# Probabilities turned by VectorE and Pool's DMAs through DRAM in a two-layer hybrid block

## The reference, cut to what matters

```
s_loc = where(ok, q @ k_loc.T * scale + bias, NEG);  s_ctx = q @ k_ctx.T * scale
p = softmax(concat([s_loc, s_ctx(, sink)]))          # rows: queries, columns: keys
o = p[:, :n_loc] @ v_loc + p[:, n_loc:] @ v_ctx
```

## Time and profile before

| What | us |
|---|---|
| median of 3 runs | 1846.57 (1845.81 to 1846.89) |
| span of the profiled execution | 1846.3 |
| TensorE busy in it | 1689.6 (92%) |
| VectorE busy | 771.0 (42%) |
| ScalarE busy | 478.0 (26%) |
| Pool busy | 111.4 (6%) |
| attention of layer 0 | about 148 to 424 |
| expert stage of layer 0 | about 580 to 1080 |
| attention of layer 1 | about 1130 to 1314 |
| expert stage of layer 1 | about 1397 to the end |

### The profile page before, as it was taken

How to read it: one execution, slowest core, us unless ns; L and a number is a source line. 1 busy time by engine, 2 the same in 40 slices (tenths; PEclk the granted TensorE clock), 3 DMA queues, 4 the chain that set the end, 5 groups by cost and what they waited for, 6 DMA issues and landing times.

```text
span 1846.3 us, 26514 instructions
## 1 busy us (share of the span) xinstructions
PE 1689.6 (92%) x10854; PEld 977.2 (53%) x10854; DVE 771.0 (42%) x1746; ACT 478.0 (26%) x1052; POOL 111.4 (6%) x149
## 2 busy tenths in 40 slices
PE   5999999999998999999898799989999997777866
PEld 2887777777674333333232398877883332222222
DVE  3455556674434233333323665577753222111111
ACT  3324455552223100000000434465441000000001
POOL 1001210000001000000000101300001000000000
PEclk8999999999998999999999999999998999999998
DMA  9532322127778999999999764337899999999996
GB/s 353 154 91 69 106 72 80 35 81 256 251 286 326 409 428 427 428 428 428 427 429 426 271 206 133 96 115 252 282 364 385 426 426 426 426 425 426 426 426 281
DMA packets 152035, 543.83 MB, mean 295 GB/s; under 512 B 10026, under 2 KB 92400, under 8 KB 126700
## 3 DMA queue, kind: packets, MB, share of 16 engines
q1 hardware_dynamic: 149104, 535.35, 74.0%
q0 software_dynamic: 2400, 6.16, 1.2%
q10 hardware_dynamic: 412, 0.64, 0.1%
HBM read 539.13 MB, written 2.98 MB: 294 GB/s over the span
## 4 chain that ended last, share of the span: by engine, by line
PE 68%; DMA 23%; DVE 4%; ACT 2%; SPq 2%; issue 1%; POOL 0%; DVEq 0%; ACTq 0%
PE bank L2158 20%; PE bank L2019 12%; PE bank L2020 11%; PE bank L2021 11%; DMA ring<-in_w_exp_down 8%; DMA ring<-in_w_exp_gate 7%; DMA ring<-in_w_exp_up 4%; DMA spare<-in_w_exp_gate 3%; PE bank L2132 2%; PE bank L2048 2%; PE bank L2071 2%; PE bank L1934 2%; PE bank L2058 2%; PE bank L2187 1%; DMA ring<-in_w_ada 1%
## 5 line engine op out<-in xcount | busy, mean ns | idle before, releaser
L2158 PE MATMUL bank<-ring,XEP 128*32 128x256 f32 (+1 forms) x2384 | 384.9, 617 | 37.1 <-DMA ring<-in_w_exp_gate 20.7
L2019 PE MATMUL bank<-HH,WH 128*128 128x512 f32 (+1 forms) x864 | 312.1, 361 | 5.7 <-DVE HL L1627 4.7
L2020 PE MATMUL bank<-HL,WH 128*128 128x512 f32 (+1 forms) x864 | 300.4, 348 | 0.0
L2021 PE MATMUL bank<-HH,WL 128*128 128x512 f32 (+1 forms) x864 | 299.9, 347 | 0.0
L2158 PEld LDWEIGHTS bank<-ring,XEP 128*32 128x32 f32 (+1 forms) x2384 | 114.1, 130 | 277.5 <-issue 227.8
L1598 DVE TENSOR_TENSOR WL<-ring,WH 128x1024 fp32r<-128x1024 f32 (+1 forms) x172 | 185.0, 1078 | 133.4 <-ACT WH L1362 132.6
L1856 DVE TENSOR_TENSOR X<-X,bank 128x512 f32<-128x512 f32 x184 | 114.0, 682 | 188.2 <-PE bank L2187 100.0
L2019 PEld LDWEIGHTS bank<-HH,WH 128*128 128x128 f32 x864 | 163.8, 190 | 54.0 <-issue 25.9
L1362 ACT CAST WH<-ring 128x1024 fp32r<-128x1024 f32 (+1 forms) x172 | 158.0, 926 | 100.5 <-PE bank L2021 64.7
L2158 PE MATMUL bank<-ring,HIDT 128*32 128x256 f32 (+1 forms) x1232 | 153.6, 481 | 31.3 <-DMA ring<-in_w_exp_down 31.3
L2021 PEld LDWEIGHTS bank<-HH,WL 128*128 128x128 f32 x864 | 163.8, 190 | 21.2
(11 more groups left out here) (244 smaller groups left out, 1955.4 us busy)
## 6 DMA issues: line engine op xcount, KB each, us to landing
ring<-in_w_exp_gate SPq DMA_DIRECT2D x55, 2048.0 KB, 30.9
ring<-in_w_exp_up SPq DMA_DIRECT2D x49, 2048.0 KB, 34.4
ring<-in_w_exp_down SPq DMA_DIRECT2D x48, 2048.0 KB, 36.6
ring<-in_w_ada SPq DMA_DIRECT2D x48, 1024.0 KB, 7.4
ring<-in_w_in SPq DMA_DIRECT2D x40, 1024.0 KB, 6.3
split_slot<-in_w_exp_up SPq DMA_DIRECT2D x8, 2048.0 KB, 29.3
split_slot<-in_w_exp_down SPq DMA_DIRECT2D x8, 2048.0 KB, 33.5
ring<-in_w_in SPq DMA_DIRECT2D x28, 512.0 KB, 5.2
```

Of the source, the lines that this page charges most:

```text
L2019: mm(t, wh, hi[:, k, 0:b.n], start=k == 0, stop=False)
L2020: mm(t, wh, lo[:, k, 0:b.n], start=False, stop=False)
L2021: last = mm(t, wl, hi[:, k, 0:b.n], start=False, stop=k == b.kk - 1)
L2158: last = mm(out_bank[tw * g:tw * g + tw, 0:nw], stationary(k), w[:, g::G] if spread else w[:, nw * g:nw * g + nw], start=k == 0, stop=k == ...
```

## The change

TensorE's transposes go. ScalarE scales PB by the reciprocal, in place, where VectorE did. A new step `swap` lets VectorE turn each 32x32 block of PB within itself and write it to a buffer PBT (one for both heads of a pair, in the last 1024 columns of the weight ring, which the ring gives up until the attention is over). Pool, at `turn`, writes PBT to one of two buffers in DRAM (`bounce`), waits until it has landed, and reads it back with four DMAs, one for each group of 32 partitions, so that the blocks lie where the transpose of the whole would put them, in PTL or PTC. TensorE waits for these DMAs (`pt_in`) before the values. The positions of the steps change: swaps come behind the normalising, values later (in layer 0 two pairs after the set's end, in layer 1 at 8/10 of the next pair's fill). Pool's bias steps are put in a new order by `bias_order`: one pair ahead in layer 0 and two in layer 1, then each next pair's behind the `turn` of a pair with a bias. The first pair of the last third of the merge does both gate blocks before the branch blocks.

```diff
         if place is None:
-            if self.top + size > STREAM[self.layer] * SLOT:
+            if self.top + size > STREAM[self.layer] * SLOT - self.kept:
                 self.top = 0
...
 
+        P.kept = PBT_W
...
@@ -582,7 +587,9 @@
                 at_ = [(both, lambda: normalise(pair[0])), (both, lambda: normalise(pair[1]))]
                 if br == "na" and last:
                     at_ = [(-(-per * 9 // 20), lambda: normalise(pair[0])), (-(-per * 7 // 10), lambda: normalise(pair[1]))]
-                at_ = sorted(at_ + [(-(-per * 3 // 10), values), (-(-per * 7 // 10), lower)], key=lambda a: a[0])
+                later = -(-per * 17 // 20) if br == "na" and last else both + 1
+                at_ += [(at_[1][0] if br == "na" and last else later, lambda: swap(pair[0])), (later, lambda: swap(pair[1]))]
+                at_ = sorted(at_ + [(-(-per * (8 if last else 4) // 10), lambda: values(pair[0].pair - (1 if last else 2))), (-(-per * (10 if last else 8) // 10), lower)], key=lambda a: a[0])
...
-
-            for st in P.turned:
-                P.add("pv", set=st)
-            P.lower += P.turned
-            P.turned = []
+        def swap(x):
+
+            P.add("swap", unit=x)
+
+        def values(until):
+
+            while P.turned and P.turned[0].end <= until + 1:
+                P.add("pv", set=P.turned[0])
...
+            P.add("turn", pair=pair)
+            if pair[1].end:
+                P.turned.append(pair[1].set)
...
-            run(atoms[:1 + KD // 2])
-            values()
-            run(atoms[1 + KD // 2:1 + KD])
-            lower()
-            run(atoms[1 + KD:mid])
+            if d2 == 0:
+                mid = 2 * KD + 3
+                atoms = atoms[:KD + 2] + atoms[KD + 8:2 * KD + 9] + atoms[KD + 2:KD + 8] + atoms[2 * KD + 9:]
+                done = 0
+                for n in (KD + 1, 2 * KD)[-len(P.turned):]:
+                    run(atoms[done:n])
+                    values(P.turned[0].end - 1)
+                    run(atoms[n:n + 3])
+                    lower()
+                    done = n + 3
+                run(atoms[done:mid])
+            else:
...
+        P.steps[l] = bias_order(out, 2 * (l + 1))
...
+def bias_order(steps, ahead):
+
+    due = [s for s in steps if s.kind == "bias"]
+    out = []
+
+    def pair():
+
+        now = [due.pop(0) for _ in range(2)] if due else []
+        out.extend(now + [Step(kind="mask", layer=s.layer, unit=s.unit) for s in now])
+
+    for s in steps:
+        if s.kind == "bias":
+            if s.unit.u == min(t.unit.u for t in steps if t.kind == "bias"):
+                for _ in range(ahead // 2):
+                    pair()
+            continue
+        out.append(s)
+        if s.kind == "turn" and s.pair[0].bias:
+            pair()
+    assert not due
+    return out
...
         RPBT = [sb(f"RPBT{l}", [8 * RPB_R, RPB_REP, RPB_C], R_O + 16384 + 8192 * l) for l in range(DEPTH)]
...
         MRG = [sb(f"MRG{l}", [128, KD, n], R_MRG) for l, n in enumerate((TOK, SEQ))]
-        PTL = sb("PTL", [128, 2, 4, SEQ], R_PT)
-        PTC = sb("PTC", [128, 2, 2, SEQ], R_PT + 8192)
+        PTL = sb("PTL", [128, 8, 2, 4, 32], R_PT)
+        PTC = sb("PTC", [128, 8, 2, 2, 32], R_PT + 8192)
+        PBT = [[sb(f"PBT{l}{nk}", [128, 4, 2, nk, 32], R_RING + 16384 * STREAM[l] - 4 * PBT_W) for nk in (4, 2)] for l in range(DEPTH)]
...
-        BLK, SB_, TB, PVB = BANK, BANK[3:5], BANK[5:7], BANK[7]
+        BLK, SB_, PVB = BANK, BANK[3:5], BANK[7]
...
+                    elif s.kind == "mask":
+                        mask(s.unit)
+                    elif s.kind == "turn":
+                        x = s.pair[1]
+                        pool.wait_ge(turn_ready, x.u + 1)
+                        run, held = 16 * x.nk // 32, bounce[x.pair % 2]
+                        if x.pair > 1:
+                            pool.wait_ge(pt_in, 64 * (x.pair - 1))
+                        pool.dma_start(held[:, 0:4 * run], PBT[l][x.set.grp][:].rearrange("p b h c j -> p (b h c j)")).then_inc(pt_out, 16)
+                        pool.wait_ge(pt_out, 16 * (x.pair + 1))
+                        if x.set.pt_before:
+                            pool.wait_ge(pv_ready, x.set.pt_before)
+                        j = x.qt % 2
+                        for b in range(4):
+                            blocks = bass.AP(tensor=held.tensor, offset=held.offset + run * b, ap=[[PBT_W, 32], [32 * PBT_W, 4], [1, run]])
+                            turned = (PTL, PTC)[x.set.grp][32 * b:32 * b + 32, 4 * j:4 * j + 4].rearrange("p a h c j -> p a (h c j)")
+                            pool.dma_start(turned, blocks).then_inc(pt_in, 16)
...
-                    elif kind == "turn":
+                    elif kind == "normalise":
                         x = s.unit
-                        act.wait_ge(turn_ready, x.u + 1)
-                        if x.set.pt_before:
-                            act.wait_ge(pv_ready, x.set.pt_before)
-                        buf, nk = (PTL, 4) if x.set.grp == 0 else (PTC, 2)
-                        j = x.qt % 2
-                        nc.scalar.copy(buf[:, x.hh, :, 128 * j:128 * j + 128],
-                                       TB[x.u % 2][:, 0:128 * nk].rearrange("p (k q) -> p k q", k=nk)).then_inc(pt_ready, 1)
+                        u2 = x.u % 2
+                        act.wait_ge(inverse_ready, x.u + 1)
+                        nc.scalar.activation(PB[u2][:, 0:x.nk], PB[u2][:, 0:x.nk], ACT.Copy, scale=RSM[u2]).then_inc(norm_ready, 1)
...
                                 link(nc.vector.tensor_reduce(MX[u2][:, 1:2], sc[:, SEQ:TOK], AX.X, ALU.max))
                                 nc.vector.tensor_reduce(NM[u2], MX[u2], AX.X, ALU.max, negate=True).then_inc(max_ready, 1)
                             elif x.br == "na":
-                                if x.u >= 2:
-                                    dve.wait_ge(turn_ready, x.u - 1)
                                 nc.vector.tensor_reduce(NM[u2], sc[:, 0:CTX], AX.X, ALU.max, negate=True).then_inc(max_ready, 1)
                             else:
-                                if x.u >= 2:
-                                    dve.wait_ge(turn_ready, x.u - 1)
                                 link(nc.vector.tensor_reduce(MX[u2][:, 0:1], sc[:, 0:CTX], AX.X, ALU.max))
...
-                        link(nc.vector.reciprocal(RSM[u2], RSM[u2]))
-                        nc.vector.tensor_scalar(PB[u2][:, 0:n], PB[u2][:, 0:n], RSM[u2], None, ALU.mult).then_inc(norm_ready, 1)
+                        nc.vector.reciprocal(RSM[u2], RSM[u2]).then_inc(inverse_ready, 1)
+                    elif kind == "swap":
+                        x = s.unit
+                        u2, n = x.u % 2, x.nk
+                        dve.wait_ge(norm_ready, x.u + 1)
+                        if x.hh == 0 and x.pair:
+                            dve.wait_ge(pt_out, 16 * x.pair)
+                        turned = PBT[l][x.set.grp][:, :, x.hh, :, :].rearrange("p b c j -> p c b j")
+                        nc.vector.transpose(turned, PB[u2][:, 0:n].rearrange("p (c b j) -> p c b j", b=4, j=32)).then_inc(turn_ready, 1)
...
                                     last.then_inc(s_ready, 1)
-                    elif kind == "turn":
-                        x = s.unit
-                        pe.wait_ge(norm_ready, x.u + 1)
-                        if x.u >= 2:
-                            pe.wait_ge(pt_ready, x.u - 1)
-                        for c in range(x.nk // 128):
-                            last = nc.tensor.transpose(TB[x.u % 2][:, 128 * c:128 * c + 128], PB[x.u % 2][:, 128 * c:128 * c + 128], IDENT)
-                        last.then_inc(turn_ready, 1)
                     elif kind == "pv":
                         st = s.set
-                        pe.wait_ge(pt_ready, st.end)
+                        pe.wait_ge(pt_in, 64 * st.end)
...
-                                last = mm(PVB[64 * hh:64 * hh + 64, 0:SEQ], v, buf[:, hh, c, :], start=c == 0, stop=c == n - 1,
+                                last = mm(PVB[64 * hh:64 * hh + 64, 0:SEQ], v, buf[:, :, hh, c, :], start=c == 0, stop=c == n - 1,
```

More of the change, by code:

```diff
@@ L205, in __init__ @@
         self.occupants = []
-        self.units = self.sets = self.biases = 0
+        self.units = self.sets = self.biases = self.pairs = 0
+        self.kept = 0
         self.mods = 0
@@ L1219, in _ @@
             waited_layer = 0
-            turned_to = []
             def mask(x):
```

31 lines of the change are left out of this document (13 added, 18 removed).

## The result

The changed kernel takes 1933.1 us (four runs, 1930.5 to 1938.8) against 1846.2 for the kernel before in the same comparison: ratio 1.048, 95% interval 1.046 to 1.050. It is 87 us slower; 29 us faster was predicted.

A forecast was written before the change was run, and what follows sets the result against it. TensorE was taken to bound the attention and DMA loads the expert stage. Gross gain 41.5 us less 6.3, 2.6 and 3.2 left 29.4: 1846.3 to 1816.9 us, 1817.2 for the median; range 1800 to 1836.

The forecast's parts named there:

- Cost zero; with that cover gone it is one scaling, 0.6 us, a pair.: Scaling moved to ScalarE: VectorE's swap waits for it, covered by evictions and weight parts; zero, or 0.6 us a pair uncovered.
- 8.8 us: A long pair's time from swap to probabilities in place: write 4.3 us plus reads 4.5 us.
- 6.3: Layer 1, neighbourhood half: Pool falls 7.8 us behind over six pairs, 1.5 is free, so 6.3 us lost.
- 2.6: Layer 0, neighbourhood half: Pool 8.4 us behind at the last, 5.8 spared before the values, so 2.6 us lost.
- 3.2 us lost: End of layer 1: only 5.6 us of work between the last pair's swap and its values, against 8.8 us.
- the smaller ring and the traffic: Weight ring loses 1024 columns, loads still fit three deep: zero; 40 MB of transfers beside the attention's loads: no cost counted.
- Hidden under TensorE except in the stretch from 1205 us: VectorE's 96 block transposes at 0.56 us add 10 us over both layers, hidden except in that layer 1 stretch.
- Rival 3: VectorE becomes the bound in layer 1, a transpose taking two passes: 6 us more, 1823 us; chance 0.06.
- Rival 1: Pool becomes the bound, each wait 1.5 us longer than taken: slower, 1869 us; chance 0.13.
- Rival 2: Pool's DMAs regularly take the longest landing, 6.5 us, as VectorE works beside them: 1947 us; chance 0.03.
- The transposes' price: TensorE's removed transposes: 0.96 us a long pair, 0.53 a short one, 39.2 us over both layers.
- The last write of layer 0: End of layer 0: the last pair is short and a k step twice as wide, so zero loss.

The follow-up runs named there:

- run 5: The changed kernel with Pool issuing the next pair's bias DMAs and doing its masks ahead of the pair's write: 1935.5 us.
- run 11: run 5 with VectorE also scaling the probabilities and swapping right behind, whole round and right data: 1892.7 us.
- run 3: The changed kernel with the write to DRAM issued from ScalarE's queue instead of Pool's: 1934.8 us.
- run 18: run 11 with the write to DRAM issued from ScalarE's queue: 1889.5 us.
- run 12: run 1 with bias ahead of the write and VectorE scaling and swapping right behind: 1855.3 us.
- run 10: The changed kernel without Pool's writes, reads and waits for them, values from other data, VectorE scaling and swapping right behind: 1832.8 us.
- run 15: run 10 without the 32 swaps (block transposes) of layer 1: 1824.9 us.
- run 6: The changed kernel with the bias ahead of the write and the write issued from ScalarE's queue: 1928.6 us.
- run 1: The changed kernel with values multiplied from a fixed buffer, TensorE not waiting for Pool's reads, the round still running: 1888.0 us.
- run 8: The change kept in the window half of layer 0 alone, the rest turned by TensorE as before: 1853.8 us.
- run 2: The changed kernel with 158 filler matmuls on TensorE before its six longest waits at the values: 1922.2 us.

## Why the prediction was wrong, point by point

- **"Cost zero; with that cover gone it is one scaling, 0.6 us, a pair."** This step failed most. The two hand-offs, and the place of the swap at a step of its own, cost 10.0 us without a round and 42.8 once the round ran and TensorE waited for it. A scaling takes 0.72 us where I took a copy's 0.59, but it isn't the duration: each hand-off stands in a queue behind casts, weight parts and exponentials, and from score to swap layer 1 takes 13.4 us on average in run 5, and 10.6 in run 11, where VectorE scales. I asked whether the waiting engine had cover, and not what the delay did to the write, from which everything else is counted.
- **"8.8 us" from swap to probabilities.** By the trace's issues and landings it was 12.1 us on average over the 32 long pairs, and 13.5 in layer 1, where I had 10.3 us of matmuls between swap and values. Of the 12.1, the write was issued 1.0 us after the swap, where I took nothing. It landed in 5.0 where I took 4.3, and Pool's first read came 0.4 behind the landing, so 5.4 after the issue; my bound for the landing was 5.1. The reads took 5.7 where I took 4.5, though their issue was right (2.19 for 2.4). The write's landing depends on what else is loaded: from issue to first read 3.5 us in the 13 long writes with under 100 KB of weights loaded meanwhile, 6.8 in the other 19. By the Trainium skill (DMA: Bandwidth & Descriptors, "Anatomy of one DMA — SWDGE (gpsimd) path") the estimate was 3.2; the trace agrees with it for quiet writes (1174.25 to 1177.45) and not for the 19. Runs 3 and 18 don't tell what a shorter way from swap to read would give, as theirs was no shorter.
- **"6.3", "2.6" and "3.2 us lost"** priced each wait once, as lateness of Pool against a steady TensorE. The table of steps shows that the prices do not add up like that. I read it as a loop, which no run isolates: a late product holds the next pair's work, whose swap waits in VectorE's queue, and so the next write. In the changed kernel TensorE's waits for the long pairs' reads add up to 58.6 us against these 12.1; in run 11 they are 40.5 and cost 37.4.
- **The swap buffer and the loads.** I called the smaller ring and the traffic zero and gave the wait for the single buffer no price. The round in the background cost 22.4 us (run 12 against run 10), nearly all of it in layer 1. Both runs have the smaller ring, so its price alone stays open.
- **The clock** had no term at all. The wait of 11.22 us was followed by the lower level, and the stretches of layer 1's attention show up to 44 us of it; filling the six longest waits gave 11 us back, net of filler that had no wait to stand in.
- **Layer 1's own room.** "Hidden under TensorE except in the stretch from 1205 us" took VectorE's swap at 0.56 us; it measured 0.70 for a long unit and 0.43 for a short one. With no round at all layer 1 was 7.2 us slower than before, where 15.4 faster was expected; run 15 puts 9.8 of that on the swaps. Rival 3 had the place right and the price (6 us) too low, as it counted VectorE's own passes and not the waits of rotated queries behind them.
- **Rivals 1 and 2.** Rival 1 came nearest in form: Pool's round 12.2 us against 10.9 was the right thing to fear, and VectorE did wait for masks in layer 0 (27.0 us). But moving the bias out of Pool's way gave nothing, and runs 6 and 18, with the write on another queue, little. With nobody waiting for the reads half of the loss stayed (run 1). So it was one of several parallel waits, not the bound. Rival 2 was rightly given little: four bias issues took 2.44 us and a mask 0.73, as before. The rule that I cited for it (the Trainium skill, SBUF — State Buffer, "SBUF: two separate sides") is hardly tested by the changed kernel, whose scalings are not on VectorE; in run 11, where they are, the 64 issues of short reads took 0.55 us in the median and 0.78 at the longest, so no run here shows more than 0.2 us of it.
- **What held.** The transposes' price: without the round layer 0 gained 16.5 of 23.8 us. The gain or loss of an attention is handed on whole: 13.7 + 71.1 - 2.4 is the 82.4 us between the spans. The last write of layer 0 was missed: I gave it zero, and run 8 shows its window half 7.0 us shorter (109.1 for 116.1 from first to last score) and the stretch behind 11.6 longer.

## What to carry to other kernels

A step that moves from one engine to a chain of four must be priced as latency through every queue that it passes, starting from where its first hand-off can happen; "hidden" has to hold for the whole chain and not for each engine. Where several waits run side by side, removing one may show nothing (the bias, the write), and the price of a part depends on which others are there (10.0 us or 42.8 for the same edit), so take them away together and put them back one at a time. A latency of this kind pays only where enough independent work lies between issue and use, as in the middle of a window half, and not at the end of a stage.

## What was not expected of the hardware

- The landing of the same 512 KB write from the same queue (Pool's) differs from run to run: medians of 4.8 us in the changed kernel, 3.6 in run 11 and 3.5 in run 2, single ones from 2.9 to 8.3 in the changed kernel. The issue takes 0.56 us on Pool and 0.33 on ScalarE.
- A wait of 11.2 us brought the granted clock to 0.50, and the 16 matmuls behind it took 3.68 us instead of 1.95. With filler in the wait the clock stayed at 1.00.
- A 32x32 block transpose of 128x512 float32 on VectorE takes 0.70 us, between one pass of that size (0.56) and two.
